# Setup and input projection of a two-block transformer kernel: three modulation parts loaded ahead of x, statistics of x in two halves, two projection units paired in one loop

## The chip, the core and the metric

The kernel runs on one core of one Trainium2 chip. The metric is the device time of one execution in microseconds, as the median of several runs. A core has five engines that run side by side and meet through semaphores: TensorE (PE in the profile) multiplies matrices, VectorE (DVE) and GpSimd (POOL) do elementwise work, ScalarE (ACT) evaluates functions and copies, SyncE (SP) issues most of the transfers from memory. ACT can issue transfers as well.

## What is computed

Two blocks of a model on x, 1024 positions of 1024 features. Only the opening of the first block matters here. A condition vector c gives six modulation rows, x is normalised and modulated, and one projection feeds three mixers:

```
mod = c @ w_ada + b_ada                  # 1024 x 6144: six rows, sh_m sc_m gt_m sh_f sc_f gt_f
h = rms_norm(x, g_pre_mix) * (1 + sc_m) + sh_m
z = h @ w_in                             # split into u (state space), f (Fourier), q, k, v (attention)
y = concat(s5_mixer(u), fourier_mixer(f), window_attention(q, k, v)) @ w_out
x = x + gt_m * rms_norm(y, g_post_mix)   # then the feed-forward part of the block, then a second block
```

The state-space mixer is a linear recurrence with complex eigenvalues (lam). Its filters are built from powers of lam times b, and its chunk carries need lam raised to powers by repeated squaring.

## The kernel before

**Modulation.** w_ada has 6144 columns, taken in twelve blocks of 512. The first four, the parts 0 to 3, are held whole: eight loads of 256 KB each, multiplied on TensorE by the condition vector spread over the array (`modulation(j)`, 16 matmuls). They come in the order 0, 2, 1, 3. Parts 0 and 2 make the shift and scale of the first half of the features, parts 1 and 3 those of the second half. The other eight blocks are weighed on VectorE (`weigh_block(b)`: eight pieces of 256 KB, each times its entries of c, added up) and summed over the partitions on TensorE (`sum_block(b)`, four small matmuls). There are two accumulators, so `weigh_block(b)` waits for `sum_block(b - 2)`. When all eight are summed, `late_modulations` on VectorE forms the remaining rows.

**x.** The eight tiles of x are loaded on ACT's queue, squared on ACT with a running sum, and their inverse root is found by one Sqrt on ACT and a few small steps on VectorE (`x_norm`). VectorE scales the first four tiles, ACT the other four. TensorE transposes x (`turn_input`), ACT applies scale and shift out of the accumulator memory (h_tmp), and VectorE splits the result into a high and a low part (`split_input`, x_hi and x_lo).

**Projection.** w_in is worked in ten units of up to 128 columns, 512 KB each. A unit has two raw buffers, two high (`win_upper`) and two low (`win_lower`) buffers for all ten: ACT casts the high part, which for unit n waits until TensorE has finished unit n - 2, and VectorE subtracts for the low part (`split(n)`). A unit is eight steps over k of three matmul pairs (`unit_step`). Unit 0 runs in the loop over x, between the transposes; units 1 to 9 follow one by one. After unit 6 come the filters, and around units 7 and 8 the transposes of the filter states (`turn_state`). `sum_block(0)` to `(3)` lie in units 3 to 6, `(4)`, `(5)` and `(6)` in unit 8, at k = 0, 2 and 6, and `(7)` at the start of unit 9.

**Order.** Everything is written out by hand: each engine runs its instructions in the order of the code, and a wait stops all that is behind it on that engine. SP's queue holds the loads of the modulation parts, the units and the pieces. The load of unit 9 stands behind the pieces of block 5, the last four of which wait until VectorE has begun to use up that block. The block's fifth piece is also behind a wait for `k_ready` 1, which VectorE raises after the squarings (`square`), just before `split(8)`. VectorE raises `k_ready` 2 with the second k_sum, and TensorE waits for that at unit 8, k = 0.

**Start of mixing.** After unit 9 TensorE spreads two modulation rows over the partitions (`spread_row`), and then starts `mix_tensor`: a small Fourier product (fw, f_t), and the transposes of u (u_t), of which the first two are free and the others wait for VectorE's copies (u_rows). VectorE reaches these copies after `fold_fourier`, `late_modulations`, and the powers of lam (`turns`, with `scale_rows` ahead of its last round).

Of the kernel before, what the change touches and what calls it, by code (L numbers as in the profile page):

```python
# [61 lines left out]
def body(ctx, nc, a, out):  # L62
# [106 lines left out]
    PIECE_0, USED_0 = 1, 2  # L169
# [29 lines left out]
    f_diff = place("f_diff", [P, HALF], RR + 10 * KB)  # L199
# [37 lines left out]

    Z_F, Z_U, Z_Q, Z_ALL = 2, 5, 8, 10
# [39 lines left out]
    def mix_tensor(pe, t):  # L278
# [72 lines left out]
        for n in range(4):  # L351
            if n % 2 == 0:
                pe.wait_ge(dft_in[n // 2], 64 if n else 32)
# [100 lines left out]
        pe.wait_ge(glu_in, 16)  # L454
# [142 lines left out]
    def mix_vector(dve, v, steps):  # L597
# [84 lines left out]
        dve.wait_ge(bias_in, 16)  # L682
# [2983 lines left out]
    def _(sp):  # L3666
# [4 lines left out]
        for j in FIRST_ORDER:  # L3671
# [4 lines left out]
        w_in = a["w_in"][0].rearrange("(k p) n -> p k n", p=P)  # L3676
# [24 lines left out]

        sp.wait_ge(vec_used, 1)
        for n in range(4):
# [15 lines left out]
    def _(act):  # L3719
# [25 lines left out]
        x = a["x"][0].rearrange("(n p) d -> p n d", p=P)  # L3745
        for n in range(NT):
            act.dma_start(x_rows[:, n, :], x[:, n, :]).then_inc(x_in, 16)

# [6 lines left out]
        act.wait_ge(x_in, 16 * NT)  # L3755
        for n in range(NT):
# [3 lines left out]
        act.wait_ge(x_var, 1)  # L3760
        nc.scalar.activation(stat_b[:, 0:NT], stat_a[:, NT:2 * NT], ACT.Sqrt).then_inc(x_std, 1)
# [3 lines left out]
        act.wait_ge(x_var, 2)  # L3765
        for n in range(NT // 2, NT):
            nc.scalar.activation(x_rows[:, n, :], x_rows[:, n, :], ACT.Identity, scale=stat_b[:, NT + n:NT + n + 1]).then_inc(x_std, 1)
# [58 lines left out]
    def x_norm(dve, v, steps):  # L3826

        dve.wait_ge(x_sq, NT)
        steps.add(v.tensor_scalar(stat_a[:, NT:2 * NT], stat_a[:, 0:NT], 1.0 / D, RMS_EPS, ALU.mult, ALU.add))
        steps.settle()  # L3830
        dve.sem_inc(x_var, 1)
        dve.wait_ge(x_std, 1)
        inverse_root(v, steps, stat_a[:, NT:2 * NT])
        dve.sem_inc(x_var, 1)
        for n in range(NT // 2):
            v.tensor_scalar(x_rows[:, n, :], x_rows[:, n, :], stat_b[:, NT + n:NT + n + 1], None, ALU.mult).then_inc(x_scaled, 1)
# [3 lines left out]
    def _(dve):  # L3840
# [9 lines left out]
        def vector_columns():  # L3850
# [3 lines left out]
            for i in range(4):  # L3854
                src = bank(4 + i // 2, wide, wide * (i % 2)).rearrange("p (g f) -> p f g", g=2)
                steps.add(v.tensor_copy(conv_cols[:, :, :, i], src))
            steps.add(v.tensor_copy(norm_cols[:].rearrange("p a k -> p (a k)"), bank(4, 2 * KD, 2 * wide)))
            steps.add(v.tensor_copy(bias_cols[:, 0:4].rearrange("p a k -> p (a k)"), bank(5, 4 * KD, 2 * wide)))
            steps.add(v.tensor_copy(bias_cols[:, 4:6].rearrange("p a k -> p (a k)"), bank(4, 2 * KD, 2 * wide + 2 * KD)))
# [200 lines left out]
        modulation_used(0)  # L4060
        modulation_used(2)
        dve.sem_inc(mod_ready, 1)
# [20 lines left out]
        dve.sem_inc(mod_ready, 1)  # L4083
        for i in range(2, 2 * KD):
            split_input(i)
            if i == 5:
# [304 lines left out]
```

## Time and profile before

| | us |
|---|---|
| median of 3 runs | 2918.99 (2918.94 to 2919.5) |
| span of the profiled execution | 2914.4 |
| outside that span | 4.6 |
| TensorE busy in the span | 2812.8 (97%) |
| VectorE busy in the span | 2102.5 (72%) |
| ScalarE busy in the span | 1331.9 (46%) |

Times in the profile are counted from the span's start. All that the change touches lies in the first 240 us. From there to the end the code is the same. In a timeline row stand the start, the time of one instruction or of a group of alike ones (x and their number), engine and line, out<-in, and in brackets how long the engine was idle before it and what ended that.

### The profile page before, as it was taken

Reading aid. Unit: us, or ns where it says so; the run is one execution under the profiler, and the core shown is the slowest. Engines: PE = TensorE matmul, PEld = TensorE weight load, DVE = VectorE, ACT = ScalarE, POOL = GpSimd, SP = SyncE. Lnnn points to the kernel's source line nnn. Section 1 sums busy time; section 2 is a strip of 40 time slices with the busy share of each in tenths; the row PEclk is TensorE's granted clock in tenths of the full one; section 3 lists DMA queues with packets and bytes.
Section 4 is the critical chain, followed back from the end, with each engine's and each line's share of the span. In section 5 each row is a group of like instructions: output and inputs, shape, how many; then the busy total and the mean of one; then the engine's idle time right before and its main releaser. Section 6 shows DMA issues by size and latency. Waiting matters only on the chain.

```text
span 2914.4 us, 37420 instructions
## 1 busy us (share of the span) xinstructions
PE 2812.8 (97%) x13573; PEld 2252.5 (77%) x13573; DVE 2102.5 (72%) x3839; ACT 1331.9 (46%) x2340; POOL 197.5 (7%) x250
## 2 busy tenths in 40 slices
PE   7998998999999999999999999999999999999997
PEld 3885677788888888888888887786677888888886
DVE  7888727988898568766666667798737866665568
ACT  3113746544444454433333453577744433333443
POOL 2050000000000000000000000223610000000000
PEclk9988999999999999999999999999999999999999
DMA  7542034244445884344447753111023354455864
GB/s 235 152 148 43 9 130 130 83 166 166 162 150 189 278 264 148 130 154 153 151 159 282 252 189 116 50 44 34 1 100 125 130 163 155 151 164 200 299 195 145
DMA packets 345430, 436.84 MB, mean 150 GB/s; under 512 B 29701, under 2 KB 191533, under 8 KB 345070
## 3 DMA queue, kind: packets, MB, share of 16 engines
q1 hardware_dynamic: 342290, 428.46, 45.1%
q10 hardware_dynamic: 2956, 5.99, 0.6%
q8 instruction: 108, 1.77, 0.2%
q14 instruction: 76, 0.62, 0.1%
HBM read 317.59 MB, written 116.50 MB: 149 GB/s over the span
## 4 chain that ended last, share of the span: by engine, by line
PE 72%; DVE 7%; ACT 2%; POOL 1%; issue 1%; DMA 0%; DVEq 0%; SPq 0%; ACTq 0%
PE psum L1993 39%; PE psum L1444 21%; PE psum L2956 4%; PE psum L1984 3%; PE psum L1084 2%; DVE count_junk L3487 1%; PE psum L3159 1%; PE psum L3146 1%; PE psum L3172 1%; PE psum L3036 0%; ACT sign_junk L3253 0%; DVE x_t L1690 0%; DVE x_b L2463 0%; POOL p_wide L3654 0%; DVE x_lo L2536 0%
## 5 line engine op out<-in xcount | busy, mean ns | idle before, releaser
L1444 PE MATMUL psum<-far_op,far_op 128*128 128x512 f32 x2772 | 629.5, 389 | 0.0
L1444 PEld LDWEIGHTS psum<-far_op,far_op 128*128 128x128 f32 x2772 | 520.1, 188 | 108.1 <-issue 0.2
L1993 PE MATMUL psum<-x_b,w_near 128*128 128x512 f32 x1440 | 346.0, 389 | 0.8 <-DVE w_near L1616 0.8
L1993 PE MATMUL psum<-x_t,w_near 128*128 128x512 f32 x1440 | 336.4, 389 | 1.7 <-ACT psum L1730 1.7
L1993 PE MATMUL psum<-x_t,w_far 128*128 128x512 f32 x1440 | 336.3, 389 | 0.0
L1993 PEld LDWEIGHTS psum<-x_t,w_near 128*128 128x128 f32 x1440 | 270.2, 188 | 58.2 <-ACT psum L1730 2.1
L1993 PEld LDWEIGHTS psum<-x_b,w_near 128*128 128x128 f32 x1440 | 270.2, 188 | 57.3 <-issue 1.2
L1993 PEld LDWEIGHTS psum<-x_t,w_far 128*128 128x128 f32 x1440 | 270.2, 188 | 56.3 <-ACT u_keep L1742 0.3
L1208 ACT CAST far_op<-far_a 128x512 fp32r<-128x512 f32 x231 | 143.9, 623 | 316.0 <-PE psum L1444 307.8
L1215 DVE TENSOR_TENSOR far_op<-far_a,far_op 128x512 fp32r<-128x512 f32 x231 | 159.7, 692 | 176.7 <-ACT far_op L1208 175.1
L1993 PE MATMUL psum<-x_b,w_far 128*128 128x512 f32 x720 | 173.1, 389 | 1.7 <-DVE val_row L1862 1.7
L1217 DVE TENSOR_TENSOR far_op<-far_b,far_op 128x512 fp32r<-128x512 f32 x231 | 159.2, 689 | 0.0
L1616 DVE TENSOR_TENSOR w_far<-w_sum,w_far 128x512 fp32r<-128x512 f32 x120 | 82.3, 686 | 106.3 <-ACT w_far L1610 106.3
L1993 PEld LDWEIGHTS psum<-x_b,w_far 128*128 128x128 f32 x720 | 135.1, 188 | 30.1 <-DVE val_row L1862 2.1
L3622 POOL TENSOR_TENSOR split_lo<-raw,split_hi 128x256 fp32r<-128x256 f32 (+1 forms) x60 | 44.8, 781 | 1619.3 <-ACT split_hi L2972 1619.3
L1209 ACT CAST far_op<-far_b 128x512 fp32r<-128x512 f32 x231 | 142.1, 615 | 0.0
L1610 ACT CAST w_far<-w_sum 128x512 fp32r<-128x512 f32 x120 | 73.9, 616 | 119.0 <-PE psum L1993 119.0
L1616 DVE TENSOR_TENSOR w_near<-w_sum,w_near 128x512 fp32r<-128x512 f32 x120 | 80.9, 687 | 64.8 <-ACT w_near L1610 64.7
L1610 ACT CAST w_near<-raw 128x512 fp32r<-128x512 f32 (+1 forms) x129 | 82.8, 642 | 72.3 <-PE psum L1993 61.3
L1616 DVE TENSOR_TENSOR w_far<-raw,w_far 128x512 fp32r<-128x512 f32 (+1 forms) x66 | 47.2, 715 | 88.7 <-ACT w_far L1610 88.7
L1061 DVE TENSOR_TENSOR src_lo<-yc_t,src_hi 128x512 fp32r<-128x512 f32 x31 | 21.4, 692 | 119.1 <-ACT w_out_hi L1054 119.1
L1984 PE MATMUL psum<-x_b,w_near 128*128 128x512 f32 x360 | 91.3, 402 | 8.5 <-DVE x_b L2301 4.1
(534 smaller groups left out, 4826.7 us busy)
## 6 DMA issues: line engine op xcount, KB each, us to landing
far_a<-row_ops SPq DMA_DIRECT2D x231, 256.0 KB, 2.9
row_ops<-hidden SPq DMA_DIRECT2D x99, 512.0 KB, 5.2
raw<-in_ffn_w SPq DMA_DIRECT2D x88, 512.0 KB, 4.4
col_sums<-hidden SPq DMA_DIRECT2D x66, 512.0 KB, 5.6
far_b<-col_sums SPq DMA_DIRECT2D x132, 256.0 KB, 3.6
raw<-in_w_up SPq DMA_DIRECT2D x44, 512.0 KB, 3.8
hidden<-in_ffn_w SPq DMA_DIRECT2D x44, 512.0 KB, 5.1
far_b<-in_ffn_w SPq DMA_DIRECT2D x66, 256.0 KB, 3.3
```

What stands on the lines that cost most here:

```text
L1084: ins = t.matmul(bank(2 * n + c), l[:, P * n:P * (n + 1)], r[:, HALF * c:HALF * (c + 1)], start=(first and m == 0), stop=(last and m == 2))
L1208: s.copy(far_a_hi[slot][:], far_a[late][t % FB][:]).then_inc(f_hi, 1)
L1209: s.copy(far_b_hi[slot][:], far_b[late][t % FB][:]).then_inc(f_hi, 1)
L1215: v.tensor_tensor(far_a_lo[slot][:], far_a[late][t % FB][:], far_a_hi[slot][:], ALU.subtract).then_inc(f_lo, 1)
L1217: v.tensor_tensor(far_b_lo[slot][:], far_b[late][t % FB][:], far_b_hi[slot][:], ALU.subtract).then_inc(f_lo, 1)
L1444: ins = t.matmul(bank(b + n), l[slot][:, rows], r[slot][:], start=(fresh and i == 0 and m == 0), stop=(i == FH - 1 and m == 2), skip_group ...
L1610: nc.scalar.copy(op_parts(p, i)[0], op_source(p, i)).then_inc(op_hi, 1)
L1616: nc.vector.tensor_tensor(lower, op_source(p, i), upper, ALU.subtract).then_inc(op_lo, 1)
L1984: ins = t.matmul(bank(b), at[:, l, cols], r, start=(first and m == 0), stop=(last and m == 2))
L1993: ins = t.matmul(bank(b), at[:, l, cols], x[:, k, r], start=(start and k == 0 and m == 0), stop=(k == 3 and m == 2), skip_group_check=not ...
L2956: ins = t.matmul(bank(2 * slot + half)[0:m], l[:, P * k:P * k + m], r[:, k, HALF * half:HALF * (half + 1)], start=(k == 0 and i == 0), sto ...
L3622: ins = g.tensor_tensor(tile_of(w_rest, m)[:, k:k + 2], tile_of(raw[slot], m)[:, k:k + 2], tile_of(w_top, m)[:, k:k + 2], ALU.subtract)
```

## The change

- SP's queue takes modulation parts 0, 2 and 1, then x (which leaves ACT's queue), then the weights of units 1 and 0, then part 3. The transposes of the small vectors (vec_rows) go ahead of modulation 2 on TensorE, and their copies (vector_columns) up on VectorE.
- The statistics of x are made in two halves of four tiles, each with its own Sqrt. VectorE scales two tiles of a half and ACT two. The first modulations stand between the halves on VectorE.
- In the loop over x, unit 1 runs two steps behind unit 0.
- `complex_step` on `lam_b_at(0)`, twelve VectorE instructions, moves from ahead of `x_norm` to behind `split(2)`. Modulation rows 1 and 3 move from ahead of the third `split_input` to behind the fourth and sixth, `split(1)` from the sixth to the second.
- A squaring takes one product of double width in place of two, and writes its imaginary part directly, without a copy.
- `split(9)` moves from behind `weigh_block(7)` to ahead of the second k_sum. `fold_fourier` moves ahead of the wait for the last sum.
- `sum_block(5)` moves to unit 8, k = 6; `(6)` and `(7)` move to unit 9, k = 2 and k = 7. `spread_row` moves into `mix_tensor`, behind the first two transposes of u.

```
-        for j in FIRST_ORDER:
...
+        for j in FIRST_ORDER[0:3]:
+            load_modulation(j)
+        for n in range(NT):
+            sp.dma_start(x_rows[:, n, :], x[:, n, :]).then_inc(x_pair_in[n // 2], 16)
+        load_unit(1)
         sp.wait_ge(vec_used, 1)
-        for n in range(4):
+        load_unit(0)
+        load_modulation(FIRST_ORDER[3])
+        for n in range(2, 4):
             load_unit(n)
...
-        complex_step(lam_b_at(0), [(b_raw[:, 0, d], b_raw[:, 1, d]) for d in range(2)], 18, 20)
-        vector_columns()
-        x_norm(dve, v, steps)
...
+        x_norm(dve, v, steps, first_modulations)
...
         split(0)
-        for i in range(2):
-            split_input(i)
-        modulation_used(1)
-        modulation_used(3)
-        dve.sem_inc(mod_ready, 1)
-        for i in range(2, 2 * KD):
+        for i in range(2 * KD):
             split_input(i)
-            if i == 5:
+            if i == 1:
                 split(1)
+            elif i == 3:
+                modulation_used(1)
+            elif i == 5:
+                modulation_used(3)
+                dve.sem_inc(mod_ready, 1)
...
+            else:
+                steps.add(v.tensor_tensor(prm[:, 22:24, :], both, both, ALU.mult))
+            steps.add(v.scalar_tensor_tensor(di, sr, 2.0, si, ALU.mult, ALU.mult))
             steps.settle()
             steps.add(v.tensor_tensor(dr, col(22), col(23), ALU.subtract))
-            steps.add(v.tensor_copy(di, col(24)))
...
         split(2)
+        complex_step(lam_b_at(0), [(b_raw[:, 0, d], b_raw[:, 1, d]) for d in range(2)], 18, 20)
         weigh_block(0)
...
         weigh_block(5)
+        split(9)
         dve.wait_ge(k_shift_in, K_SHIFT_0 + 16)
...
-        split(9)
+        fold_fourier(dve, v, steps)
         dve.wait_ge(ada_mm, N_ADA)
-        fold_fourier(dve, v, steps)
         late_modulations()
...
+                elif j == 3 and k in (4, 7):
+                    turn_half(0, k // 7)
...
             ins = unit_step(0, k)
...
+            if k >= LAG:
+                unit_step(1, k - LAG)
+        for k in range(KD - LAG, KD):
+            ins = unit_step(1, k)
...
-                elif n == 8 and k in (0, 2, 6):
+                elif n == 8 and k in (0, 6):
...
-                elif n == 9 and k == 0:
-                    sum_block(7)
+                elif n == 9 and k in (2, 7):
+                    sum_block(6 + k // 7)
...
+            if i == 2:
+                for row in range(2):
+                    spread_row(row)
```

VectorE from `split(2)` (win_lower_109) to `split(3)` (win_lower_110); ada_acc is a block being weighed, w_tmp and lam_b the powers of lam. Before:

```order
L4067 TENSOR_TENSOR win_lower_109<-win_raw_105,win_upper_107 128x1024 [waits win_hi]
L4019 TENSOR_SCALAR ada_acc_76<-ada_piece_72,c_cols 128x512 [waits vec_used]
...
L4022 SCALAR_TENSOR_TENSOR ada_acc_76<-ada_piece_75,c_cols,ada_acc_76 128x512 [waits x_var,prm_lam]
L3974 TENSOR_TENSOR w_tmp<-lam_b,prm 128x192 [waits x_var]
...
L4067 TENSOR_TENSOR win_lower_110<-win_raw_106,win_upper_108 128x1024 [waits win_hi,dve_steps]
```

And now:

```order
L4101 TENSOR_TENSOR win_lower_109<-win_raw_105,win_upper_107 128x1024 [waits win_hi]
L4008 TENSOR_TENSOR w_tmp<-b_raw,prm 128x192
...
L4016 TENSOR_TENSOR lam_b<-w_tmp 128x12x16 [waits dve_steps]
...
L4053 TENSOR_SCALAR ada_acc_76<-ada_piece_72,c_cols 128x512 [waits vec_used,dve_steps]
...
L4056 SCALAR_TENSOR_TENSOR ada_acc_76<-ada_piece_75,c_cols,ada_acc_76 128x512 [waits x_var,prm_lam]
L4008 TENSOR_TENSOR w_tmp<-lam_b,prm 128x192 [waits x_var]
...
L4101 TENSOR_TENSOR win_lower_110<-win_raw_106,win_upper_108 128x1024 [waits win_hi,dve_steps]
```

The twelve instructions on b_raw and w_tmp now stand between the two splits, with block 0 and the next power of lam behind them.

VectorE from the end of block 5 (ada_acc_77) to the first modulation row (mod_sum); win_lower_110 is `split(9)`, the k_sum from k_shift raises `k_ready` 2. Before:

```order
L4022 SCALAR_TENSOR_TENSOR ada_acc_77<-ada_piece_75,c_cols,ada_acc_77 128x512 [waits x_var,prm_lam]
L4135 TENSOR_TENSOR k_sum<-psum,k_shift 128x384 [waits x_var,k_shift_in]
L4019 TENSOR_SCALAR ada_acc_76<-ada_piece_72,c_cols 128x512 [waits vec_used,ada_mm]
...
L4138 MEMSET fw_rows 128x256 [waits x_var]
L4067 TENSOR_TENSOR win_lower_110<-win_raw_106,win_upper_108 128x1024 [waits dve_steps,win_hi]
L589 TENSOR_TENSOR f_diff<-f_t 128x511 [waits z_ready,ada_mm]
...
L4030 TENSOR_TENSOR mod_sum<-psum,bias_cols 128x32 [waits dve_steps,ada_mm]
```

And now:

```order
L4056 SCALAR_TENSOR_TENSOR ada_acc_77<-ada_piece_75,c_cols,ada_acc_77 128x512 [waits x_var,prm_lam]
L4101 TENSOR_TENSOR win_lower_110<-win_raw_106,win_upper_108 128x1024 [waits x_var,win_hi]
L4171 TENSOR_TENSOR k_sum<-psum,k_shift 128x384 [waits k_shift_in]
L4053 TENSOR_SCALAR ada_acc_76<-ada_piece_72,c_cols 128x512 [waits vec_used,ada_mm]
...
L4174 MEMSET fw_rows 128x256 [waits x_var]
L593 TENSOR_TENSOR f_diff<-f_t 128x511 [waits dve_steps,z_ready]
...
L4064 TENSOR_TENSOR mod_sum<-psum,bias_cols 128x32 [waits dve_steps,ada_mm]
```

`split(9)` now stands ahead of the k_sum that TensorE waits for, and the fold (f_diff) no longer waits for the last sum (ada_mm); mod_sum still does.

TensorE from the end of unit 8 (win_lower_109) through unit 9 (win_upper_108, win_lower_110) to the transposes of u; one_cols with ada_acc is a `sum_block`, row_cols a `spread_row`. Before:

```order
L4302 MATMUL psum<-x_hi,win_lower_109 128x512 x2
L4231 MATMUL psum<-one_cols,ada_acc_77 128x1 [waits ada_used,z_ready,win_lo]
...
L4302 MATMUL psum<-x_hi,win_lower_110 128x512 x2
L4242 MATMUL psum<-ident,row_cols_79 128x128 [waits win_ready,c_spread]
...
L284 MATMUL psum<-fw_rows,dft_d 128x128 [waits z_ready,fw_in]
...
L307 MATMUL psum<-ident,u_t 128x128 x8
L307 MATMUL psum<-ident,u_t 128x128 [waits u_rows_ready]
```

And now:

```order
L4339 MATMUL psum<-x_hi,win_lower_109 128x512 x2
L4339 MATMUL psum<-x_hi,win_upper_108 128x512 [waits z_ready,win_lo]
...
L4269 MATMUL psum<-one_cols,ada_acc_76 128x1 [waits ada_used]
...
L4269 MATMUL psum<-one_cols,ada_acc_77 128x1 [waits ada_used]
...
L285 MATMUL psum<-fw_rows,dft_d 128x128 [waits z_ready,fw_in]
...
L311 MATMUL psum<-ident,u_t 128x128 x8
L4280 MATMUL psum<-ident,row_cols_79 128x128 [waits win_ready,c_spread]
...
L311 MATMUL psum<-ident,u_t 128x128 [waits u_rows_ready]
```

The last sum has gone from the first instruction of unit 9 to its last step, and the spread rows from ahead of the Fourier product to behind two transposes of u.

## Rows read from the trace of the kernel before

**Rows 1.** The page's first line.

```profile
span 2914.4 us, 37420 instructions
```

**Rows 2.** TensorE's waits to 240 us: line, waited for: total, times, longest.

```profile
PE psum L4210 <- DMA ada_w<-in_w_ada: 12.9, 3, 8.3
...
PE psum L4302 <- DVE x_lo L4075: 4.8, 4, 2.5
```

**Rows 3.** Windows: length, TensorE busy (x), granted clock, DMA share, GB/s.

```profile
31.70:36.40 4.70, 4.69 (x6) 0.51 1.06 389
31.70:43.10 11.40, 11.39 (x23) 0.80 0.86 316
43.10:52.70 9.60, 9.60 (x26) 1.00 0.68 221
56.60:78.90 22.30, 17.47 (x99) 1.00 0.22 72
78.90:89.80 10.90, 10.90 (x49) 1.00 0.61 184
```

**Rows 4.** TensorE's timeline: parts 1 and 3, a transpose of x, the loop's start.

```profile
41.18 11.33 PE L4210 MATMUL psum<-ada_w,c_bcast 128*128 128x512 f32 x26
...
55.80 1.04 PE L4224 MATMUL psum<-ident,x_rows 128*128 128x128 f32 x8
56.59 0.70 PE L4302 MATMUL psum<-x_hi,win_upper 128*128 128x512 f32 x2
```

**Rows 5.** VectorE's timeline: first of complex_step, split(2), next power of lam, split(3).

```profile
31.36 0.64 DVE L3974 TENSOR_TENSOR w_tmp<-b_raw,prm 128x192 f32<-128x192 f32 x1
...
80.21 1.22 DVE L4067 TENSOR_TENSOR win_lower<-win_raw,win_upper 128x1024 fp32r<-128x1024 f32 x1 [2.83 <-ACT win_upper L3778]
...
89.40 0.36 DVE L3974 TENSOR_TENSOR w_tmp<-lam_b,prm 128x192 f32<-128x192 f32 x1
...
92.88 1.22 DVE L4067 TENSOR_TENSOR win_lower<-win_raw,win_upper 128x1024 fp32r<-128x1024 f32 x1
```

**Rows 6.** Window of GpSimd: length, busy (x), granted clock, DMA share, GB/s.

```profile
60.00:100.00 40.00, 0.00 (x0) 1.00 0.43 135
```

**Rows 7.** VectorE by line and form, the squarings, 151.9 to 165.6 us: busy, mean ns.

```profile
L4095 DVE COPY pw<-prm 128x24 f32<-128x24 f32 x9 | 2.1, 236 | 0.0
L4091 DVE TENSOR_TENSOR prm<-pw 128x24 f32<-128x24 f32 x8 | 1.8, 226 | 0.0
```

**Rows 8.** Timelines of VectorE, SP, TensorE and ACT around units 8 and 9.

```profile
167.69 1.31 DVE L4067 TENSOR_TENSOR win_lower<-win_raw,win_upper 128x1024 fp32r<-128x1024 f32 x1
...
172.90 0.43 SPq L3684 DMA_DIRECT2D win_raw<-in_w_in  x1
...
176.88 0.56 DVE L4135 TENSOR_TENSOR k_sum<-psum,k_shift 128x384 f32<-128x384 f32 x1
...
179.66 0.95 PE L4231 MATMUL psum<-one_cols,ada_acc 128*128 128x1 f32 x8
...
179.86 1.05 ACT L3778 CAST win_upper<-win_raw 128x1024 fp32r<-128x1024 f32 x1 [0.80 <-PE psum L4302]
...
198.84 1.05 PE L4231 MATMUL psum<-one_cols,ada_acc 128*128 128x1 f32 x8 [1.87 <-DVE win_lower L4067]
```

**Rows 9.** DMA issues from 165 to 180 us: unit 9, us from issue to landing.

```profile
win_raw<-in_w_in SPq DMA_DIRECT2D x1, 512.0 KB, 5.9
```

**Rows 10.** The raw units' tile: all loads from issue to landing.

```profile
DMA to landing us min/median/max: 4.0/4.7/9.9
```

**Rows 11.** Timelines of VectorE and TensorE from the late modulations to u_rows.

```profile
203.87 0.19 DVE L4030 TENSOR_TENSOR mod_sum<-psum,bias_cols 128x32 f32<-128x32 f32 x1
...
215.09 1.22 DVE L4044 TENSOR_TENSOR row_a<-row_a,psum 128x1024 f32<-128x1024 f32 x1
...
224.68 1.29 DVE L601 COPY u_rows<-psum 128x512 f32<-128x512 f32 x2
...
225.42 1.31 PE L307 MATMUL psum<-ident,u_t 128*128 128x128 f32 x8 [2.26 <-DVE u_rows L601]
```

More of the change, by code:

```diff
@@ L198, in body @@
     yf_odd = place("yf_odd", [P, 2, HALF], XR + 28 * KB)
-    f_diff = place("f_diff", [P, HALF], RR + 10 * KB)
+    f_diff = place("f_diff", [P, HALF], RR + 16 * KB)
     u_rows = place("u_rows", [P, GROUPS, CH, GC], RR)
@@ L3752, in _, with square_input @@
         nc.scalar.activation(prm[:, 11, :], prm[:, 7, :], ACT.Sin, scale=0.5).then_inc(prm_trig, 1)
-        act.wait_ge(x_in, 16 * NT)
-        for n in range(NT):
+        def square_input(n):
+            act.wait_ge(x_pair_in[n // 2], X_PAIR)
             if n:
@@ L3759, in _, with input_root, scale_input @@
             nc.scalar.activation(junk[:], x_rows[:, n, :], ACT.Square, accum_out=stat_a[:, n:n + 1]).then_inc(x_sq, 1)
-        act.wait_ge(x_var, 1)
-        nc.scalar.activation(stat_b[:, 0:NT], stat_a[:, NT:2 * NT], ACT.Sqrt).then_inc(x_std, 1)
+        def input_root(half):
+            act.wait_ge(x_var, 2 * half + 1)
+            cols = slice(HN * half, HN * (half + 1))
+            nc.scalar.activation(stat_b[:, cols], stat_a[:, NT + cols.start:NT + cols.stop], ACT.Sqrt).then_inc(x_std, 1)
+        def scale_input(half):
+            act.wait_ge(x_var, 2 * half + 2)
+            for n in range(HN * half + 2, HN * half + 4):
+                nc.scalar.activation(x_rows[:, n, :], x_rows[:, n, :], ACT.Identity, scale=stat_b[:, NT + n:NT + n + 1]).then_inc(x_std, 1)
+        for n in range(4):
+            square_input(n)
+        act.sem_inc(x_in, 16 * NT - X_PAIR)
+        input_root(0)
+        for n in range(4, 6):
+            square_input(n)
+        scale_input(0)
+        for n in range(6, 8):
+            square_input(n)
+        input_root(1)
+        scale_input(1)
         act.dma_start(row_a[:], a["g_post_mix"].to_broadcast([P, D])).then_inc(bc_in, 16)
@@ L3824, in inverse_root, with x_norm @@
         steps.settle()
[L3826 to L3836, printed above, removed]
+    def x_norm(dve, v, steps, between):
+        for half in range(2):
+            cols, var = slice(HN * half, HN * (half + 1)), stat_a[:, NT + HN * half:NT + HN * (half + 1)]
+            dve.wait_ge(x_sq, HN * (half + 1))
+            steps.add(v.tensor_scalar(var, stat_a[:, cols], 1.0 / D, RMS_EPS, ALU.mult, ALU.add))
+            steps.settle()
+            dve.sem_inc(x_var, 1)
+            dve.wait_ge(x_std, 3 * half + 1)
+            inverse_root(v, steps, var, cols)
+            dve.sem_inc(x_var, 1)
+            for n in range(HN * half, HN * half + 2):
+                v.tensor_scalar(x_rows[:, n, :], x_rows[:, n, :], stat_b[:, NT + n:NT + n + 1], None, ALU.mult).then_inc(x_scaled, 1)
+            if half == 0:
+                between()
     @block.vector
@@ L4313, in _ @@
             ins = unit_step(0, k)
+            if k == KD - 1:
+                ins.then_inc(win_mm, 1)
+            if k == LAG:
+                pe.wait_ge(win_lo, 2)
+                pe.wait_ge(c_ready, 2)
+                pe.wait_ge(vec_used, 1)
+            if k >= LAG:
+                unit_step(1, k - LAG)
+        for k in range(KD - LAG, KD):
+            ins = unit_step(1, k)
         ins.then_inc(win_mm, 1)
-        for n in range(1, len(win_units)):
+        for n in range(2, len(win_units)):
             pe.wait_ge(win_lo, n + 1)
@@ L4335, in _ @@
                 filters()
-        for i in range(2):
-            spread_row(i)
-        mix_tensor(pe, t)
+        mix_tensor(pe, t, spread_row)
 def constants():
```

88 lines of the change are left out of this document (42 added, 46 removed).

## The prediction

> **What bounds the kernel now.** Read the page's first line, then TensorE's waits over the opening, then the timelines around each long wait. The profiled execution spans 2914.4 us [rows 1], 4.6 us under the median of 2918.99. The change ends at about 240 us and the code behind is untouched, so I ask when the mixing starts and add that shift to the median. The opening is a chain that changes hands. TensorE waits 8.3 us for a modulation part, then 4.8 us in the loop over x for VectorE's low parts [rows 2]; it is busy without a gap through unit 1 [rows 3], waits 1.87 us for split(9) [rows 8], and 2.26 us for the first copy of u_rows [rows 11]. The last of these counts most: TensorE resumes at 225.42, 0.74 us after the copy began at 224.68, and VectorE has been in one run of work since 203.87, when the late modulations began [rows 11]. Whatever delays these delays the mixing by as much.
>
> **Step 1, loads.** Parts 0, 2 and 1 no longer share the queues with x, so the 8.3 us go [rows 2]. But part 3 now comes after x and two units. Before, it was in by 43.1, since TensorE's window to there has no gap. Ahead of it stand two units more, 1.05 MB: at 316 GB/s 3.3 us, at 389 GB/s 2.7, at 221 GB/s, the rate of the stretch in which these units came before, 4.7 [rows 3]. I take 3.3, so 46.4 (45.8 to 47.8). TensorE is done with the other three parts before that, some 10 us: a wait of that size takes the place of the 8.3. Part 3 is 16 matmuls at 11.33 / 26 = 0.43, 6.9 us; the two half transposes beside it and the next transpose up to the loop are 1.04 + 0.79 = 1.8 [rows 4]. After the wait of 8.3 the granted clock was 0.51 for 4.7 us, which is the lower level, 1.2 GHz [rows 3]; the same costs 4.7 / 2 = 2.35. The loop starts at 46.4 + 6.9 + 1.8 + 2.35 = 57.5, against 56.59: +0.9. Without the slow stretch it is 55.1.
>
> The Trainium skill (TensorE: Matmul & The Clock Gate, The HAM clock gate) says the array runs at half rate until it has been busy again for a while. It speaks against trading one wait for another that ends nearer the loop: by it the loop starts at 57.5, without it at 55.1. The half-rate row behind the 8.3-us wait agrees.
>
> The two halves of the statistics, the vectors and the queue that x leaves cost nothing: part 3 comes in after x, and its transposes need the scaled x only from 46.4 + 4 x 2 x 0.43 on. If that cover is gone, a later x delays the loop one for one.
>
> **Step 2, the loop.** It takes 22.3 us with 17.5 busy; a unit is 10.9, or 1.36 a step [rows 3]. Unit 0's last step now has five steps of unit 1 ahead of it: 17.5 + 6.8 = 24.3. The waits of 4.8 shrink, since TensorE has more work per step from k = 2, but VectorE still does two modulation rows and a split between the first low parts: 0 to 4.8, I take 2. Unit 0 ends at 57.5 + 26.3 = 83.8, and unit 1 three steps later at 87.9, against 89.8: 1.9 us gained for TensorE. But split(2) waits for the end of unit 0, which was 78.9 and is 83.8, so split(2) goes from 80.21 to 85.1 [rows 5]: 4.9 us lost for VectorE, which has then been idle.
>
> **Step 3, VectorE's stretch.** From split(2) at 80.21 to split(8) at 167.69 are 87.5 us [rows 5, 8]. The moved complex_step is added. Where it stood one instruction took 0.64; the same shapes took 0.36 at 89.40, and twelve of them 92.88 - 89.40 = 3.5 [rows 5]. GpSimd does nothing from 60 to 100 [rows 6], so I take 3.5; twelve at 0.64 would be up to 7.7.
>
> The Trainium skill (SBUF — State Buffer, Who interferes with whom) says that a VectorE instruction with two inputs from this memory contends with a GpSimd one that reads it. By it 3.5 holds while GpSimd is idle, and 7.7, so 4.2 more in the sum, if GpSimd works there.
>
> The squarings lose nine copies, 2.1 us, and at most eight second products, 1.8 [rows 7]; a product of double width gives some back. 1.4 to 3.9, I take 3. split(8) comes at 167.7 + 4.9 + 3.5 - 3 = 173.1. On the way split(3) ends at 85.1 + 12.7 + 3.5 + 1.2 = 102.5, and TensorE, through unit 2 at 87.9 + 10.9 = 98.8, waits 3.7 us: the gain of step 2 is gone there.
>
> **Step 4, the second k_sum.** TensorE waits for it at unit 8, k = 0; at 179.66 it was ready, having been made at 176.88 [rows 8]. Now split(9) stands ahead of it. split(9) needs ACT's cast of unit 9, that needs the load, and SP issues the load 172.90 - 167.69 = 5.2 us after split(8), since block 5 must be used up first. The load took 5.9 [rows 9], others 4.0 at least [rows 10]. So 5.2 + 5.9, cast 1.05, split 1.23, k_sum 0.56 [rows 8], and 0.1 for each of three hand-overs: 14.2. Unit 8 starts at 173.1 + 14.2 = 187.3 instead of 179.66: +7.6. TensorE has unit 7 done before that, so what it does in between doesn't count. Queued behind the waiting split(9) are k_sum and block 6 on VectorE, and behind TensorE's wait all of unit 8.
>
> **Step 5, the last sum.** Before, sum 7 was unit 9's first instruction at 198.84, and the late modulations began at 203.87, after the fold. Unit 8 took 179.66 to 196.97 (198.84 less the wait), and has one sum fewer now, 0.8: 16.5. Unit 9 starts at once, the 1.87 us are saved: sum 6, 0.8, seven steps, 9.5, sum 7, 0.95. The late modulations begin at 187.3 + 16.5 + 11.3 = 215.1, against 203.87: +11.2. The fold is done by then. VectorE's 20.8 us from there to u_rows stay [rows 11]. Spreading the rows behind the transposes gains nothing: it moves into a wait that gets longer. They are needed 11.2 us behind 215.09, at 226.3; TensorE, done with unit 9 at 216.5, reaches them some 7 us later and needs 3.7: 227.2, late for the second row by less than the first scaling's 1.22.
>
> **Sum.** 2914.4 + 4.6 + 11.2 = 2930.2. In parts: unit 0's later end +4.9, complex_step +3.5, squarings -3, split(9) ahead of k_sum +2.2 (14.2 against the 12.0 from split(8) to unit 8 before), and +3.6 between unit 8 and the late modulations. Bounds: part 3 -0.6 and +1.4, half rate -2.35, loop waits -2 and +2.8, squarings -0.9 and +1.6, the load -1.9; a slow stretch in unit 8 after its wait, +2.35. All low 2922.5, all high 2938.4; complex_step's +4.2 would come on top, and GpSimd's empty window speaks against it.
>
> **Rivals.** (a) VectorE keeps up: split(8) stays at 167.7 because its waits for pieces absorb the delay, and only steps 4 and 5 act: unit 8 at 181.9, the late modulations at 209.7, +5.8: 2924.8 (2922 to 2926.5). For it: VectorE was idle 2.83 us before split(2) [rows 5]. Against: that idle time is the wait for unit 0, which moves. (b) Faster: TensorE's waits set the time, the loop's 4.8, 1.87 and 2.26 go: 2919 - 8.9 = 2910. It decides at the late modulations: to lose nothing they must begin by 203.9, so unit 8 by 176.1 and split(8) by 161.9, 11.2 us ahead of step 3. Nothing in the rows gives that. (c) More waits, more slow clock: after the waits at units 3 and 8 and the 10 us or so at u_t TensorE restarts at half rate, each 2.35, and the loop keeps its 4.8: 2934 to 2942. For it: the row behind the 8.3-us wait. Against: the loop's four waits, up to 2.5 long, left the clock at 1.00 [rows 2, 3]. (d) Pairing fills nothing, because the low parts pace the loop throughout: the loop keeps 4.8, +2.8: 2933, inside the forecast.
>
> **Chances.** Forecast with (d), 2926.5 to 2934: 0.53. (a) 0.20. (c) 0.17. (b) 0.05. No change, 2914 to 2922: 0.05. 2922 to 2938 holds the forecast, (a) and half of (c), 0.81. This measurement can tell 0.2%, 5.8 us, from no change: slower than 2924.8 are the forecast, (c) and half of (a), 0.80; within are the other half of (a) and no change, 0.15; faster (b), 0.05.
>
> **What would show it.** TensorE's waits: L4210 one of about 10 us ahead of part 3; the loop's under 4.8; a new one on win_lower at unit 3 of 3 to 4 us; one on k_sum at unit 8 of 4 to 8; u_rows above 8. VectorE: split(2) near 85, split(8) near 173, the late modulations near 215. Wrong if split(8) comes before 169, if unit 8 starts before 183, if VectorE is not idle ahead of the late modulations, or if a wait further on takes the shift up.

## The result and the profile after

The changed kernel takes 2931.91 us in the median of four runs (2930.86 to 2933.29), the one before 2919.24 beside it (2918.94 to 2921.06). The ratio is 1.0049, with a 95% interval from 1.0037 to 1.0061: 14.3 us more, 10.8 to 17.8. The forecast was 2930.2, in a range from 2922 to 2938.

The profiled execution took 2933.29 us:

```profile
span 2931.5 us, 37423 instructions
```

That is 17.1 us more than [rows 1], while TensorE resumes the transposes of u 14.8 us later than in [rows 11]. The other 2.3 us come behind that, far from the change, where stretches of half-rate clock lie differently in the two runs: 1.6 of them appear at one place, where the granted clock is 0.67 from 1819 to 1824 us in the changed kernel and 1.00 in the like stretch of the one before, from 1802 to 1807. The spans of the four runs reach from 2929.1 to 2931.5. Executions that ran disturbed, at a lower clock, are left out of all times, and as the profiled one of run e7 below was such, nothing is read from its trace.

TensorE's waits to 260 us, longest totals first (columns as in [rows 2]). The one cut out in the middle is 5.2 us in both kernels, and four short ones of the mixing are left out at the end:

```profile
PE psum L4245 <- DMA ada_w<-in_w_ada: 14.2, 3, 10.3
PE psum L311 <- DVE u_rows L605: 8.9, 1, 8.9
...
PE psum L4339 <- DVE win_lower L4101: 4.9, 2, 3.0
PE psum L4269 <- DVE k_sum L4171: 4.0, 1, 4.0
PE psum L4339 <- DVE x_lo L4109: 2.2, 3, 1.1
PE psum L285 <- ACT v_t L3813: 1.2, 1, 1.2
```

Against [rows 2] the wait for a modulation part has grown from 8.3 to 10.3 and the loop's for low parts have shrunk from 4.8 to 2.2. Four are new or larger: win_lower at units 3 and 6, k_sum at unit 8, v_t ahead of the Fourier product, and u_rows, 8.9 where [rows 11] has 2.26. Waits alone don't say what set the end. For that VectorE's timeline is read, from split(2) through the first complex_step instruction to split(3), and then around units 8 and 9:

```profile
83.91 1.22 DVE L4101 TENSOR_TENSOR win_lower<-win_raw,win_upper 128x1024 fp32r<-128x1024 f32 x1 [2.84 <-ACT win_upper L3807]
85.05 0.35 DVE L4008 TENSOR_TENSOR w_tmp<-b_raw,prm 128x192 f32<-128x192 f32 x1
...
99.50 1.23 DVE L4101 TENSOR_TENSOR win_lower<-win_raw,win_upper 128x1024 fp32r<-128x1024 f32 x1
...
172.42 1.31 DVE L4101 TENSOR_TENSOR win_lower<-win_raw,win_upper 128x1024 fp32r<-128x1024 f32 x1
...
185.32 1.50 DVE L4101 TENSOR_TENSOR win_lower<-win_raw,win_upper 128x1024 fp32r<-128x1024 f32 x1 [3.64 <-ACT win_upper L3807]
186.74 0.55 DVE L4171 TENSOR_TENSOR k_sum<-psum,k_shift 128x384 f32<-128x384 f32 x1
...
217.83 0.19 DVE L4064 TENSOR_TENSOR mod_sum<-psum,bias_cols 128x32 f32<-128x32 f32 x1 [3.72 <-PE psum L4269]
...
229.60 1.22 DVE L4078 TENSOR_TENSOR row_a<-row_a,psum 128x1024 f32<-128x1024 f32 x1 [0.56 <-DVE turn L585]
231.33 1.22 DVE L4078 TENSOR_TENSOR row_b<-row_b,psum 128x1024 f32<-128x1024 f32 x1 [0.51 <-PE psum L4280]
```

Four rows of [rows 5, 8, 11] are answered here: split(2) is 3.7 us later (80.21), split(3) 6.6 (92.88), split(8) 4.7 (167.69), and the late modulations (mod_sum) 14.0 (203.87). In between VectorE waits 3.64 us for the cast of unit 9, with k_sum queued behind it, and 3.72 us for the last sum. TensorE on the same stretch, at part 3, the loop's start, unit 3, unit 8 with its sum, sum 7, the Fourier product, the spread rows and the transposes of u:

```profile
45.30 5.62 PE L4245 MATMUL psum<-ada_w,c_bcast 128*128 128x512 f32 x8 [10.30 <-DMA ada_w<-in_w_ada]
...
56.42 0.73 PE L4339 MATMUL psum<-x_hi,win_upper 128*128 128x512 f32 x2 [0.32 <-DVE x_lo L4109]
...
100.78 1.22 PE L4339 MATMUL psum<-x_hi,win_upper 128*128 128x512 f32 x2 [3.04 <-DVE win_lower L4101]
...
187.54 1.84 PE L4269 MATMUL psum<-one_cols,ada_acc 128*128 128x1 f32 x8 [4.00 <-DVE k_sum L4171]
...
216.77 0.95 PE L4269 MATMUL psum<-one_cols,ada_acc 128*128 128x1 f32 x8
...
220.42 1.13 PE L285 MATMUL psum<-fw_rows,dft_d 128*128 128x128 f32 x8 [1.19 <-ACT v_t L3813]
...
227.56 3.74 PE L4280 MATMUL psum<-ident,row_cols 128*128 128x128 f32 x32
240.24 1.97 PE L311 MATMUL psum<-ident,u_t 128*128 128x128 f32 x8 [8.94 <-DVE u_rows L605]
```

A sum of eight narrow products takes 1.84 us at 187.54 and 0.95 at 216.77. Windows of the changed kernel behind the wait for part 3, behind the wait at unit 3, over the end of the wait for k_sum and over the work behind it (length; busy and count of TensorE, weight loads, VectorE, ScalarE, GpSimd; granted clock, DMA share, GB/s) say why:

```profile
45.30:49.20 3.90, 3.90 (x5) 1.83 (x6) 2.10 (x3) 2.53 (x3) 0.00 (x0) 0.50 0.80 267
100.40:103.80 3.40, 3.02 (x9) 2.44 (x9) 2.98 (x6) 0.00 (x0) 0.00 (x0) 0.50 0.45 122
...
185.72:187.54 1.82, 0.00 (x0) 0.03 (x1) 1.56 (x2) 0.00 (x0) 1.82 (x3) 0.50 0.02 8
187.54:192.55 5.01, 5.01 (x18) 4.47 (x19) 2.82 (x4) 0.59 (x1) 4.78 (x9) 0.50 0.21 57
```

The granted clock falls to 0.50, 1.2 GHz, during the wait for k_sum and stays there through the first 5.01 us of unit 8. Behind the waits for part 3 and at unit 3 it is down too.

### The profile page after: what moved, and what is told of

The parts are those of the page before. It is cut to its first block, busy times and chain, and to the rows that moved or that the text cites. A ratio compares the mean times of both kernels' runs of the same rounds, so it can differ in the third digit from the quotient of the medians.

```text
span 2931.5 us, 37423 instructions
## 1 busy us (share of the span) xinstructions
PE 2815.0 (96%) x13573; PEld 2253.4 (77%) x13573; DVE 2100.1 (72%) x3828; ACT 1331.5 (45%) x2341; POOL 197.3 (7%) x250
## 4 chain that ended last, share of the span: by engine, by line
PE 71%; DVE 7%; ACT 2%; POOL 1%; issue 1%; DMA 1%; DVEq 0%; SPq 0%; ACTq 0%
PE psum L1997 38%; PE psum L1448 20%; PE psum L2960 4%; PE psum L1988 3%; PE psum L1088 2%; DVE count_junk L3491 1%; PE psum L3163 1%; PE psum L3150 1%; PE psum L3176 1%; PE psum L3040 0%; ACT sign_junk L3257 0%; DVE x_t L1694 0%; DVE x_b L2467 0%; POOL p_wide L3658 0%; PE psum L2628 0%
## 5 line engine op out<-in xcount | busy, mean ns | idle before, releaser
L1997 PE MATMUL psum<-x_b,w_far 128*128 128x512 f32 x720 | 173.1, 389 | 1.7 <-DVE val_row L1866 1.7
```

The lines of the kernel that those rows point to most:

```text
L1997: ins = t.matmul(bank(b), at[:, l, cols], x[:, k, r], start=(start and k == 0 and m == 0), stop=(k == 3 and m == 2), skip_group_check=not ...
```

## The experiments

**The theory.** VectorE's one chain sets the start of the mixing: split(2), complex_step, split(8), the load and cast of unit 9, split(9), k_sum, TensorE's unit 8, the last sum, the late modulations, the powers of lam, the copies of u. Each link later moves the end. **The rivals:** VectorE takes delays up in its waits and only the late sums count; or the shift is TensorE's, from more waits and half-rate clock. Each kernel undoes one part of the change, or does one alone. The table sets two readings of each beside one another: when TensorE resumes the transposes of u in the profiled run, against 225.42 in [rows 11], and the time by the ratio to the kernel before on the same chip.

| kernel | transposes of u, us | time, us (95%) |
|---|---|---|
| the change | +14.8 | +14.3 (10.8 to 17.8) |
| e1, sums and spread rows back | +6.6 | +7.0 (4.4 to 9.6) |
| e2, complex_step back in front | +11.0 | +11.4 (7.9 to 15.2) |
| e3, units 0 and 1 not paired | +12.4 | +11.7 (7.9 to 15.5) |
| e4, k_sum ahead of split(9) | +9.0 | +11.7 (7.9 to 15.2) |
| e5, before with sum 7 late | +8.5 | +10.5 (6.4 to 14.6) |
| e6, before with the squarings | +1.3 | -0.6 (-3.2 to 2.0) |
| e7, front parts alone | no reading | +1.2 (-1.5 to 3.8) |
| e8, front parts, unpaired | +1.9 | -1.2 (-3.8 to 1.2) |
| e9, before with filters dealt out | -1.0 | +2.0 (-0.6 to 4.7) |
| e10, a version built on these | -4.5 | -5.8 (-8.5 to -3.2) |
| e11, sums back, spread rows late | +14.6 | +14.0 (10.5 to 17.8) |

Of eleven readings at the transposes nine lie inside the interval of the time; e8 and e9 lie 0.7 and 0.4 us outside. So within these intervals what happens by 240 us is what the kernel's time shows. The intervals of e2, e3 and e4 overlap with that of the change: what these three parts are worth is read from the traces alone. A trace is one execution. Up to the loop's start the change, e1, e3, e4 and e11 have the same code, and the loop starts between 56.42 and 57.52 us; in the kernel before, e5, e6, e9 and e10 it starts between 54.13 and 57.16. Readings of 1 or 2 us at the transposes (e6, e8, e9) are therefore not told from none.

**e1: the sums and the spread rows back where they were**, the rest of the change kept.

```
-                elif n == 8 and k in (0, 6):
+                elif n == 8 and k in (0, 2, 6):
...
-                elif n == 9 and k in (2, 7):
-                    sum_block(6 + k // 7)
+                elif n == 9 and k == 0:
+                    sum_block(7)
...
-                for row in range(2):
-                    spread_row(row)          # in mix_tensor, behind two transposes
+        for i in range(2):
+            spread_row(i)                    # ahead of mix_tensor
```

> The changed kernel with the sums of blocks 5 to 7 and the spread rows back at the places they had before; all else as changed. Theory (the chain of VectorE through the late modulations sets the end): unit 8 still starts near 187.5. Block 7 can be weighed from about 197.5, right behind block 6, to 205.5; the last sum runs at the start of unit 9 near 206.5; the fold ends near 209.8 and the late modulations begin there, 8 us before the 217.8 of the changed kernel. Time 2932 - 8 = 2924 (2922 to 2926). Rival (the opening loads and the loop set the end, the late sums are hidden): within 1 us of 2932.

Measured +7.0 us, 2924.61 in the median. The late modulations, in VectorE's timeline of e1, and the resumed transposes, in TensorE's:

```profile
210.41 0.19 DVE L4061 TENSOR_TENSOR mod_sum<-psum,bias_cols 128x32 f32<-128x32 f32 x1 [0.22 <-DVE f_t L594]
```

```profile
232.00 1.31 PE L308 MATMUL psum<-ident,u_t 128*128 128x128 f32 x8 [1.98 <-DVE u_rows L602]
```

The first were at 217.83, the second at 240.24. So about half of the loss is in the late end of the sums and rows, half ahead of it: the first rival, that only the late sums count, is out.

**e2: complex_step back in front of the statistics of x.**

```
+        complex_step(lam_b_at(0), [(b_raw[:, 0, d], b_raw[:, 1, d]) for d in range(2)], 18, 20)
         x_norm(dve, v, steps, first_modulations)
...
         split(2)
-        complex_step(lam_b_at(0), [(b_raw[:, 0, d], b_raw[:, 1, d]) for d in range(2)], 18, 20)
```

> The changed kernel with complex_step on lam_b_at(0) back ahead of the statistics of x. Theory: the twelve instructions, 3.5 us, leave the stretch from split(2) to split(8), the wait of 3.0 us at unit 3 goes, split(8) comes near 169 instead of 172.4 and all behind follows: 2932 - 3.5 = 2928.5 (2927 to 2930). Rival (TensorE sets the pace there, VectorE has slack): no change, 2932, with split(8) earlier but unit 8 not.

TensorE's timeline of e2, unit 8's sum and the resumed transposes:

```profile
183.58 1.84 PE L4269 MATMUL psum<-one_cols,ada_acc 128*128 128x1 f32 x8 [4.18 <-DVE k_sum L4171]
...
236.46 3.84 PE L311 MATMUL psum<-ident,u_t 128*128 128x128 f32 x16 [8.94 <-DVE u_rows L605]
```

split(3) comes at 96.63, split(8) at 169.41, unit 8 at 183.58 and the transposes at 236.46, 2.9 to 4.0 us earlier than with the change, the transposes 3.8. The delay of twelve instructions at 85 us is still there, undiminished, at 240: VectorE's waits on the way don't absorb it.

**e3: unit 1 after unit 0, not beside it.**

```
-        LAG = 2
+        LAG = KD
...
-            if k == LAG:
+            if k == KD - 1:
                 pe.wait_ge(win_lo, 2)
```

> The changed kernel with unit 1 behind unit 0 again, not in the loop over x. Theory: unit 0 ends some 4 us earlier, split(2) comes near 80 instead of 83.9, split(8) near 168.5, and the end moves by the same: 2928 (2926.5 to 2930), although TensorE ends unit 1 about 2 us later and waits in the loop for 4 to 5 us instead of 2.2. Rival (pairing gains as TensorE's time): 2 us slower, 2934.

split(2) comes 2.3 us earlier, at 81.61, where 80 was expected. The loop happened to start 1.1 us later in this run (57.52); counted from its start, split(2) is 3.4 us earlier. Unpaired, the loop's waits for low parts are 5.3 us, above the 4.8 of [rows 2]. split(8) comes 3.6 us earlier (168.84), unit 8 3.1 (184.44), the transposes 2.5 where 4 were expected. So pairing delays VectorE nearly by the 4.0 us that step 2 of the prediction holds for it (6.8 of unit 1 less 2.8 of waits), and by less at the end. And a bound shows that the theory had left out: ahead of k_shift VectorE waits for TensorE's filters (VectorE's timeline of e3, split(2) and k_shift; L4320 is the filters' line).

```profile
81.61 1.22 DVE L4101 TENSOR_TENSOR win_lower<-win_raw,win_upper 128x1024 fp32r<-128x1024 f32 x1 [2.83 <-ACT win_upper L3807]
...
166.68 0.38 DVE L4158 MEMSET k_shift<- 128x384 f32 x1 [0.54 <-PE psum L4320]
```

**e4: k_sum ahead of split(9).**

```
         weigh_block(5)
-        split(9)
         dve.wait_ge(k_shift_in, K_SHIFT_0 + 16)
         v.tensor_tensor(k_sum[:, 0, :], bank(0, taps), k_shift[:], ALU.add).then_inc(k_ready, 1)
+        split(9)
```

> The changed kernel with split(9) right behind the second k_sum instead of ahead of it. Theory: the 4.0 us that TensorE waits for k_sum at unit 8 go, unit 8 starts near 183.5, the half-rate stretch behind that wait may go too (6.8 us of it cost 3.4), and nothing else moves: 2926 to 2928.5. Rival (unit 9's weights are then late, since split(9) waits for the same load): 2932, the wait turning up at unit 9.

TensorE's timeline of e4, unit 8's sum and the resumed transposes:

```profile
184.10 0.95 PE L4269 MATMUL psum<-one_cols,ada_acc 128*128 128x1 f32 x8
...
234.37 3.87 PE L311 MATMUL psum<-ident,u_t 128*128 128x128 f32 x16 [8.93 <-DVE u_rows L605]
```

The wait of 4.00 is gone, unit 8 begins 3.44 us earlier, and the clock stays at 1.00 (184.10 to 211.00), so the sum takes 0.95. From unit 8's start to sum 7 are 26.8 us here (184.10 to 210.91) and 29.2 in the changed kernel (187.54 to 216.77): the half-rate stretch costs 2.4. Together 5.9, all of it at the transposes. Of the second rival, that the shift is TensorE's, these 2.4 us of half-rate clock hold; e1 and e2 rule it out for the rest. split(9) still waits 2.52 us for the cast; no one waits for it now.

**e5: the kernel before, with only the last sum at unit 9's last step.**

```
-                elif n == 9 and k == 0:
+                elif n == 9 and k == 7:
                     sum_block(7)
```

> The kernel before with one thing moved: the last sum goes from the start of unit 9 to its last step. Theory: the last sum ends at 198.8 + 9.5 + about 2 = 210 to 211, the fold still follows it, the late modulations begin at 214 to 215 instead of 203.9 and TensorE's wait for u_rows grows from 2.3 to about 13: 2919 + 11 = 2930 (2928 to 2932). Rival (TensorE's other work covers it): 2919 to 2922.

TensorE's timeline of e5, sum 7, the spread rows and the transposes:

```profile
207.40 0.95 PE L4231 MATMUL psum<-one_cols,ada_acc 128*128 128x1 f32 x8
...
213.30 6.76 PE L4242 MATMUL psum<-ident,row_cols 128*128 128x128 f32 x32 [3.44 <-DVE row_cols L4033]
...
233.88 3.87 PE L307 MATMUL psum<-ident,u_t 128*128 128x128 f32 x16 [6.75 <-DVE u_rows L601]
```

One line moved by seven steps costs 10.5 us. Behind the wait of 3.44 the spread rows take 6.76 us instead of 3.73, at half rate again: the granted clock is 0.54 from 213.30 to 220.00. So the wait at u_rows is not the expected 13 us but 6.75; most of the rest lies ahead of it. The late sum makes VectorE late (8.5 us at the transposes), and no other part of the change is needed for that.

**e6: the kernel before, with only the shorter squarings.**

```
-            steps.add(v.tensor_tensor(col(22), sr, sr, ALU.mult))
-            steps.add(v.tensor_tensor(col(23), si, si, ALU.mult))
-            steps.add(v.scalar_tensor_tensor(col(24), sr, 2.0, si, ALU.mult, ALU.mult))
+            steps.add(v.tensor_tensor(prm[:, 22:24, :], both, both, ALU.mult))
+            steps.add(v.scalar_tensor_tensor(di, sr, 2.0, si, ALU.mult, ALU.mult))
...
-            steps.add(v.tensor_copy(di, col(24)))
```

> The kernel before with the shorter squarings alone. Theory: split(8) comes 2.9 us earlier, near 164.8, but k_ready 1 and the second k_sum were not waited for in the kernel before, so VectorE waits that much longer for the sum of block 4: 2919, within 1.5. Rival (VectorE sets the pace through units 8 and 9): 2916.

No change, as expected, but not for the reason given. VectorE's timeline of e6 behind the last squaring:

```profile
165.88 0.38 DVE L4123 MEMSET k_shift<- 128x384 f32 x1 [3.51 <-PE psum L4283]
```

What the squarings save, VectorE waits for the filters. In the changed kernel this wait is not there, because VectorE comes later: k_shift starts at 170.25, and the filters' last product had started at 168.9. So the squarings are worth something only where VectorE is late or the filters are early.

**e7 and e8: the front parts alone.** e7 has the loads, statistics, pairing, squarings and the early fold, with the sums, spread rows and split(9) as before and complex_step in front. e8 is that, unpaired, with split(9) moved between blocks 6 and 7.

```
# e8 against e7
-        LAG = 2
+        LAG = KD
...
         weigh_block(6)
+        split(9)
         weigh_block(7)
...
-        split(9)
         fold_fourier(dve, v, steps)
```

> The changed kernel with its later parts undone: sums, spread rows, split(9) and complex_step back at the places of before. What is left is the order of loads, the halves of the statistics, the pairing, the squarings and the fold ahead of the last sum. Theory: split(2) 3.7 later than before, squarings 2.9 shorter, so split(8) within 1 us of 167.7; the fold, 3.9 us, off the path behind the last sum: 2916 to 2920. Rival (the pairing costs VectorE what it costs in the changed kernel): 2922 or more.

> As the run with the later parts undone, but with unit 1 behind unit 0 again, and split(9) between blocks 6 and 7. Theory: split(2) near 80, split(8) near 164.5, no wait at unit 9 (1.87 before), the fold off the path: late modulations 3 to 6 us earlier than 203.9, but the spread rows then set when the rows are scaled: 2914 to 2917. Rival (TensorE's half-rate stretches eat it): 2918 to 2920.

Neither moves the time: +1.2 (-1.5 to 3.8) and -1.2 (-3.8 to 1.2). Of e8 2 to 5 us less had been expected. The reason that the expectation gives for e7, a later split(2) against shorter squarings, stays open, as no trace of e7 is read. VectorE's timeline of e8 at k_shift:

```profile
166.71 0.38 DVE L4155 MEMSET k_shift<- 128x384 f32 x1 [2.62 <-PE psum L4317]
```

VectorE waits 2.62 us for the filters (L4317), until 166.71, and split(8) stands at 168.90, 1.2 us behind [rows 8]. The filters' 96 narrow products start from 148.0 to 164.2 in the kernel before and from 148.9 to 166.1 in e8: TensorE comes to them no earlier by the new loads, and VectorE can't pass them.

**e9: the kernel before, with the filters dealt out** over unit 7's first four steps, 24 products each, instead of 96 in one run ahead of unit 7.

```
-            if n == 6:
-                filters()
...
+                if n == 7 and k < 4:
+                    filters(k, 4)
```

> The kernel before with one thing changed: the 96 filter matmuls, which run in one block behind unit 6 with a granted clock of 0.50, are dealt out in four parts ahead of the first four steps of unit 7. Theory (the narrow matmuls by themselves bring the clock down): between wide matmuls the clock stays at 1.00, filters and four steps take about 16.5 us instead of 24.3, TensorE then waits for k_ready near 167.6 and for k_sum near 177.5, and unit 8 starts there instead of at 179.7: 2 us faster than before. Rival (the clock falls all the same): no change, within 1.5 us of before.

Nothing measurable, where 2 us less were expected. A window of the kernel before from 4.4 us behind the start of the filters to 5.0 us into unit 7, and one of e9 over the whole stretch that holds them (columns as above; the granted clock is the third number from the end):

```profile
152.40:169.40 17.00, 17.00 (x70) 15.94 (x70) 16.13 (x48) 1.96 (x2) 16.30 (x29) 0.50 0.13 47
```

```profile
63.80:166.10 102.30, 97.65 (x507) 82.35 (x505) 84.98 (x195) 19.90 (x23) 24.01 (x39) 1.00 0.48 144
```

Dealt out, the filters run at the full clock. But TensorE then waits 5.04 us at 167.94 for VectorE's first k_sum (its timeline in e9):

```profile
167.94 1.12 PE L4297 MATMUL psum<-ident,lam_b 128*128 128x128 f32 x4 [5.04 <-DVEq L4131]
```

Behind this wait it runs at 0.50 again, from 168.00 to 173.00. VectorE waits 2.6 to 3.5 us for the filters where it is early (e6, e8), TensorE 5.0 us for VectorE where the filters are early: whoever frees one of the two meets the other.

**e10: both freed, and what follows them.** The kernel before, with the filters of e9, the squarings of e6, split(9) between blocks 6 and 7, and the fold ahead of the wait for the last sum. The buffer f_diff moves by 6 KB, since it shared its place with an accumulator of the blocks, which is still in use at the earlier fold.

```
         weigh_block(6)
+        split(9)
         weigh_block(7)
...
-        split(9)
-        dve.wait_ge(ada_mm, N_ADA)
         fold_fourier(dve, v, steps)
+        dve.wait_ge(ada_mm, N_ADA)
         late_modulations()
```

> The kernel before with the filters dealt out over unit 7, the shorter squarings, split(9) between blocks 6 and 7, and the fold ahead of the wait for the last sum; loads, loop, complex_step, sums and spread rows as before. Theory: split(8) near 165, k_sum near 174.5, unit 8 near 175 instead of 179.7, no wait at unit 9 and the fold off the path: u_rows 6 to 8 us earlier, so 6 us faster than before (4 to 8). Rival (the clock falls in the filters all the same): 1 to 3 us faster.

It takes 2912.98 us against 2917.55, a ratio of 0.9980 (0.9971 to 0.9989): faster than both kernels, each taken by its ratio to the kernel before. Two timelines of e10, VectorE's with split(8) and the late modulations, and TensorE's with its two waits in units 7 and 8 and the resumed transposes:

```profile
165.95 1.31 DVE L4067 TENSOR_TENSOR win_lower<-win_raw,win_upper 128x1024 fp32r<-128x1024 f32 x1
...
199.31 0.19 DVE L4030 TENSOR_TENSOR mod_sum<-psum,bias_cols 128x32 f32<-128x32 f32 x1 [0.22 <-DVE f_t L593]
```

```profile
165.92 0.65 PE L4297 MATMUL psum<-ident,lam_b 128*128 128x128 f32 x4 [0.93 <-DVEq L4131]
...
176.14 1.20 PE L4231 MATMUL psum<-one_cols,ada_acc 128*128 128x1 f32 x8 [2.68 <-DVE k_sum L4135]
...
220.90 3.71 PE L307 MATMUL psum<-ident,u_t 128*128 128x128 f32 x16 [3.32 <-DVE u_rows L601]
```

split(8) is 1.7 us earlier than in [rows 8] and 2.0 earlier than in e9 (167.97), which has the filters dealt out but not the squarings; the late modulations are 4.6 earlier than in [rows 11]. Which of the four edits carries how much wasn't taken apart, and e9 shows only that the filters alone give nothing.

**e11: the changed kernel with the sums back and the spread rows left late.** Its diff is the first half of e1's.

> The changed kernel with the sums of blocks 5 to 7 back at the places of before, the spread rows left behind the first transposes of u. Theory: the late modulations begin near 210 as in the run with both moved back, but the spread rows now come only behind the Fourier product, at about 228 to 232; VectorE's scaling waits for them, and so do its last round and u_rows: 10 to 12 us slower than before, against 8 with the spread rows moved back too. Rival (the spread rows are covered wherever they stand): 8 us slower than before.

It is as slow as the change, +14.0 us; the rival that the expectation names, that late spread rows cost little by themselves, is out. VectorE's timeline of e11, the late modulations and the first scaled row, and TensorE's, the spread rows:

```profile
210.42 0.19 DVE L4064 TENSOR_TENSOR mod_sum<-psum,bias_cols 128x32 f32<-128x32 f32 x1 [0.22 <-DVE f_t L597]
...
229.43 1.22 DVE L4078 TENSOR_TENSOR row_a<-row_a,psum 128x1024 f32<-128x1024 f32 x1 [7.78 <-issue]
```

```profile
227.38 3.74 PE L4280 MATMUL psum<-ident,row_cols 128*128 128x128 f32 x32
```

The late modulations are 7.4 us earlier and the scaling begins at the same time, since the spread rows now come late by themselves. Late sums cover late spread rows, so taking the sums back alone gives nothing; with the rows taken back too (e1) it gives 8.2 us at the transposes. And by e5, in the kernel before, a late sum 7 costs as much without late spread rows. The spread rows alone were not taken back in any run.

## Why the prediction was right

**Step 1, loads.** Right. Part 3 was awaited until 45.30 (forecast 46.4), after a wait of 10.30 (some 10), and the loop began at 56.42 (57.5). The half-rate stretch behind the wait was there, 3.90 us at 0.50. That is what the Trainium skill (TensorE: Matmul & The Clock Gate, The HAM clock gate) says, and the side on which the prediction had put it.

**Step 2, the loop.** Right. Waits of 2.2 (2), split(2) at 83.91 (85.1), early by what the loop's start was early. TensorE was done with unit 1 at 86.7 (87.9). Counted from the loop's start, in e3 unpaired TensorE is done with it 3.4 us later and VectorE's split(2) comes 3.4 us earlier (4.0): the gain of the one engine is the loss of the other.

**Step 3, VectorE's stretch.** Right. complex_step took 0.35 an instruction, 3.5 us, with GpSimd idle, and e2 finds them again at the end (3.8). The squarings fell from 13.7 us (151.9 to 165.6) to 10.85 (159.31 to 170.16), 2.85 less (3). split(8) at 172.42 (173.1), 1.0 us more behind split(2) than before (0.5), and the wait of TensorE at unit 3, 3.04 (3.7). A second one, 1.83 us at unit 6, was not forecast; it lies off the chain.

**Step 4, the second k_sum.** Right in place and size: unit 8 at 187.54 (187.3). That it is so close is luck in part: split(2) came 1.2 us earlier than forecast, and the way from there to split(8) took 0.5 more and from split(8) to unit 8 0.9 more (15.1 for 14.2). The load of unit 9, issued 5.3 us behind split(8), landed after 6.4 (5.9):

```profile
177.72 0.43 SPq L3690 DMA_DIRECT2D win_raw<-in_w_in  x1
...
win_raw<-in_w_in SPq DMA_DIRECT2D x1, 512.0 KB, 6.4
```

(The first of these rows is from SP's timeline of the changed kernel, the second from its DMA issues, 165 to 190 us.) **The mis-sized term** is here. The sum had nothing for a half-rate clock behind this wait; the bounds had 2.35. It came and cost 2.4, as e4 shows. The step went by the loop's waits of up to 2.5, which had left the clock at 1.00. The wait, forecast at 4 to 8 us, lay between that row and the other one, the 8.3 us behind which the clock was at 0.51 [rows 2, 3], and the step took the milder without a reason. The kernel before has a nearer row, which the prediction doesn't use: behind its wait of 1.87 us at unit 9 the clock was down too, there without harm, since sum 7 came first (window of the kernel before, columns as above).

```profile
200.20:203.60 3.40, 3.40 (x10) 2.62 (x9) 3.23 (x6) 0.00 (x0) 0.00 (x0) 0.50 0.08 17
```

In the changed kernel the wait of 1.83 us at unit 6 left the clock at 1.00 (139.00 to 145.00). So in these runs the length of a wait doesn't tell by itself what the clock does behind it.

**Step 5, the last sum.** Right in kind, 2.7 us short: the late modulations at 217.83 (215.1). Of these 2.4 are the half-rate stretch and 0.2 unit 8's later start. The fold was done by then, as forecast: VectorE waited 3.72 us. Two things were left out behind it. The spread rows had lain ahead of the Fourier product and covered ACT's copy of v; without them TensorE waits 1.19 us there. That and unit 9's later end bring both spread rows in late: VectorE waits 0.56 us ahead of the first scaling (row_a; the first row's last product ends 0.1 us before it) and 0.51 ahead of the second, where it waited 0.21 ahead of the second alone before. Its stretch from the late modulations to the resumed transposes is 22.4 us long, 0.9 more than in [rows 11]. The step had put this delay at nothing: it had only the second row late, by less than a scaling.

**Sum and rivals.** 4.9 + 3.5 - 3 + 2.2 + 3.6 gave +11.2. At the transposes it is +14.8: 2.4 for the clock, 0.2 for unit 8, 0.9 behind the late modulations. Rival (a), VectorE keeps up, is out by split(8) and e2; (b) never came near; (c) is true of the clock, which fell behind all three waits that it named; of these stretches one, in unit 8, lay on the path to the transposes. The one behind them (0.50 from 240.24 to 243.70) has a like in the kernel before (0.50 from 227.6 to 234.3), and the one at unit 3 is off the chain. The loop didn't keep its 4.8, so (d) is out. What the prediction didn't see is that the filters bind VectorE at 166 us as soon as it is a few us early. That is why the squarings alone gain nothing (e6), and the front parts without the late ones (e8) no more.

## What to carry to other kernels

When instructions of an in-order queue are moved behind a wait or to a later step, follow the one chain that ends at the next stage and price every link, then ask of each row ahead of a moved one what it had been covering. Undo moved parts in pairs as well as one by one: here late sums and late spread rows cost about 8 us together, and taking back the sums alone gave nothing. A stage with two bounds a few us apart pays only when both move; find the second one in the trace of the first experiment, before giving the idea up.

## What was not expected of the hardware

TensorE ran at 1.2 GHz without having waited. In the kernel before it was busy throughout the 17.00 us from 152.40 to 169.40, and the granted clock is 0.50: the first 12 of them are narrow products of 128x32, of which 4.4 us had already run, and the last 5 wide ones of 128x512. The same 96 narrow products, dealt out 24 at a time between wide ones, left it at 1.00 (e9, windows above). Here being busy was not enough for the full clock. Why that is so no run here tells.
